# A block of attention mixers and a mixture of experts on one core: two more places for streamed weights, and another order in the experts' one-chunk items

## The reference, cut to what matters

```python
def moe_swiglu(h, router_w, w_gate, w_up, w_down):      # h: 256 x 1024
    logits = (h @ router_w).astype(jnp.float32)          # 8 experts
    top_logit, top_idx = lax.top_k(logits, TOP_K)        # TOP_K = 2
    gate = jax.nn.softmax(top_logit, axis=-1)
...
    def expert_block(args):
        tok, e = args
        xb = h[tok]
        hid = jax.nn.silu(xb @ w_gate[e]) * (xb @ w_up[e])   # 1024 x 3584 each
        return hid @ w_down[e]                               # 3584 x 1024
...
    return jnp.zeros_like(h).at[row_token].add(y)
```

## The kernel before

| item | 0 | 1 | 2 | 3 | 4 | 5 | 6 | 7 | 8 | 9 | 10 |
|---|---|---|---|---|---|---|---|---|---|---|---|
| chunks | both | 0 | both | both | both | 1 | 0 | 1 | 1 | both | 0 |
| groups | 3 | 1 | 3 | 3 | 3 | 1 | 4 | 1 | 4 | 3 | 1 |

## Time and profile before

### The profile page before, as it was taken

How to read it: one execution, slowest core, us unless ns; L and a number is a source line. 1 busy time by engine, 2 the same in 40 slices (tenths; PEclk the granted TensorE clock), 3 DMA queues, 4 the chain that set the end, 5 groups by cost and what they waited for, 6 DMA issues and landing times.

```text
span 2036.8 us, 44518 instructions
## 1 busy us (share of the span) xinstructions
PE 1910.4 (94%) x19574; PEld 1226.8 (60%) x19574; DVE 757.2 (37%) x1757; ACT 332.6 (16%) x772; POOL 292.3 (14%) x266
## 2 busy tenths in 40 slices
PE   6999988999999999999988899799999999999995
PEld 4886556578888888886777645235344453544352
DVE  5586547346553554436566510110100110111102
ACT  3005635121000000213453300000000000000001
POOL 0872614000000000076341000000000000000000
PEclk8999989999999999999899799999999999999997
DMA  9224672422213222321202799999999999999995
GB/s 355 84 83 151 222 248 86 167 82 83 84 63 104 83 83 78 131 83 42 83 2 86 296 354 393 411 418 414 418 419 418 419 396 421 371 415 397 369 406 246
DMA packets 134573, 481.93 MB, mean 237 GB/s; under 512 B 11770, under 2 KB 48490, under 8 KB 103530
## 3 DMA queue, kind: packets, MB, share of 16 engines
q1 hardware_dynamic: 129904, 473.99, 59.8%
q0 software_dynamic: 928, 3.15, 0.5%
q10 hardware_dynamic: 3546, 1.91, 0.3%
HBM read 476.92 MB, written 2.10 MB: 235 GB/s over the span
## 4 chain that ended last, share of the span: by engine, by line
PE 69%; DMA 3%; POOL 3%; DVE 3%; ACT 1%; issue 1%; DVEq 0%; SPq 0%; ACTq 0%; POOLq 0%
PE bank L837 67%; DMA ring<-in_moe_w_dram 3%; PE bank L840 2%; POOL ring L3644 2%; POOL work L3646 1%; DVE gates L3561 1%; ACT ring L1965 1%; POOL work L3642 0%; DVE hT L3565 0%; ACT L1965 0%; DVE small L2767 0%; DVE ring L2948 0%; DVE ring L2967 0%; DVE ring L2824 0%; DVE ring L2977 0%
## 5 line engine op out<-in xcount | busy, mean ns | idle before, releaser
L837 PE MATMUL bank<-ring,hT 128*32 128x256 f32 (+3 forms) x9664 | 790.1, 472 | 34.8 <-DMA ring<-in_moe_w_dram 19.5
L837 PEld LDWEIGHTS bank<-ring,hT 128*32 128x32 f32 (+1 forms) x9664 | 343.8, 113 | 468.6 <-issue 330.6
L837 PE MATMUL bank<-ring 64*64 64x64 f32 (+5 forms) x4184 | 420.3, 298 | 31.2 <-ACT ring L1965 11.3
L837 PEld LDWEIGHTS bank<-ring 64*64 64x64 f32 (+3 forms) x4184 | 345.1, 161 | 92.6 <-issue 46.5
L837 PE MATMUL bank<-hT,ring 128*128 128x256 f32 (+1 forms) x1448 | 363.4, 407 | 6.0 <-DMA ring<-in_w_in_dram 2.8
L837 PEld LDWEIGHTS bank<-hT,ring 128*128 128x128 f32 x1448 | 278.0, 194 | 75.8 <-issue 35.0
L1965 ACT ACTIVATE gates<-bank 128x256 f32<-128x256 f32 (+2 forms) x75 | 36.2, 484 | 704.3 <-PE bank L837 686.6
L3561 DVE TENSOR_TENSOR gates<-gates,bank 128x512 f32<-128x512 f32 (+1 forms) x42 | 25.1, 597 | 280.3 <-PE bank L837 280.3
L3584 DVE COPY work<-bank 128x512 f32<-128x512 f32 (+1 forms) x18 | 9.4, 554 | 279.9 <-PE bank L837 279.9
L3726 POOL DMA_INDIRECT table<-token_rows,moe_index x10 | 9.2, 921 | 705.6 <-PE bank L840 580.8
L3546 DVE SCALAR_TENSOR_TENSOR xT<-bank,mods,xT 128x256 f32<-128x256 f32 x88 | 35.5, 476 | 178.7 <-PE bank L837 178.7
(11 more groups left out here) (268 smaller groups left out, 1403.0 us busy)
## 6 DMA issues: line engine op xcount, KB each, us to landing
ring<-in_moe_w_dram SPq DMA_DIRECT2D x240, 1024.0 KB, 19.7
ring<-in_moe_w_dram SPq DMA_DIRECT2D x128, 768.0 KB, 16.7
ring<-in_ada_w_dram SPq DMA_DIRECT2D x24, 2048.0 KB, 7.9
ring<-in_ffn_w_dram SPq DMA_DIRECT2D x22, 1024.0 KB, 7.6
ring<-in_w_in_dram SPq DMA_DIRECT2D x10, 2048.0 KB, 8.9
ring<-in_w_out_dram SPq DMA_DIRECT2D x4, 2048.0 KB, 9.5
ring<-in_ffn_w_dram SPq DMA_DIRECT2D x4, 1536.0 KB, 6.3
ring<-in_ffn_w_dram SPq DMA_DIRECT2D x4, 1280.0 KB, 5.8
```

Source lines behind the costliest of these rows:

```text
L837: return nc.tensor.matmul(o, w, x, start=start, stop=stop)
```

## The change

- `fixed_places` (new) puts each piece into the ring or into one of two **side places** of 8 KB a partition, whichever comes free earlier by the count of used pieces. The two are `work[:, 0:2 * D]` (where `hrow`, the rows for item 0's gather, lay) from the first used piece on, and `spare` from the 17th used piece on.
- SP waits for the store of `hrow` to `token_rows` ahead of the first piece that goes to `work`.
- `fetched` is now one buffer in `work`. GpSimd fetches item u's rows when item u - 1's rows have been turned.
- `pick` moves to `tmpA`, and a scratch of the routing to `cond`.
- One-chunk items: TensorE does `turn_spread` and `next_rows` ahead of the down; `next_rows` waits for the first two groups' products and no longer for all. VectorE makes the picks ahead of `multiply(0)`.
- All items: the first piece of a down goes group by group, each group's matmuls behind a wait for that group alone.
- A count of 20 semaphores for the pieces, where it was 19; the loop for overflowing experts, which doesn't run with these inputs, loads `hrow` again.

```diff
-PIECE_SEMS = 19
+PIECE_SEMS = 20
+SIDE_FREE = (1, 2 * DT + 1)
...
-        pick = work[:, 3072:3328]
-        wpick = work[:, 3328:4352]
-        spread = work[:, 4352:5376]
+        wpick = work[:, 3072:4096]
+        spread = work[:, 4096:5120]
+        fetched = work[:, 5120:6144]
+        pick = tmpA[:, 256:512]
...
-        def fetched(u):
-            return spare[:, u % 2 * D:u % 2 * D + D]
+        side = (work[:, 0:2 * D], spare)
...
+        def fixed_places(order):
+
+            got, at, free = [], RING_FROM, list(SIDE_FREE)
+            for n, (kind, c, b) in enumerate(order):
+                size = words(kind, c)
+                if at % RING + size > RING:
+                    start = at + RING - at % RING
+                else:
+                    start = at
+                need = max((k + 1 for k, (where_to, lo, _) in enumerate(got) if where_to is None and lo < start + size - RING), default=0)
+                s = free.index(min(free))
+                if free[s] < need:
+                    got.append((s, 0, free[s]))
+                    free[s] = n + 1
+                else:
+                    got.append((None, start, need))
+                    at = start + size
+            return got
...
                     else:
+                        if first_item and n == first_in_rows:
+                            sp.wait_ge(rows_stored, 32)
                         sp.wait_ge(moe_used, before_load(u, n))
...
-                        if b == 0:
-                            pe.wait_ge(moe_hidT_ready, done0 + (i + 1) * G)
...
-                        for q in range(2):
-                            for g in range(G):
-                                for s in range(4):
...
+                        by_group = [(q, g) for g in range(G) for q in range(2)]
+                        for q, g in by_group if b == 0 else sorted(by_group):
+                            if (b, q) == (0, 0):
+                                pe.wait_ge(moe_hidT_ready, done0 + (i * G + g + 1))
+                            for s in range(4):
...
-                        pe.wait_ge(moe_hid_ready, done0 + len(cs) * G)
+                        pe.wait_ge(moe_hid_ready, done0 + (len(cs) - 1) * G + min(G, 2))
...
-                    down(0, {4: turn_spread, 5: next_rows})
+                    turn_spread()
+                    next_rows()
+                    down(0)
...
+                if len(cs) == 1:
+                    next_picks()
                 multiply(0)
...
-                if u > 2:
-                    pool.wait_ge(moe_gathered, 2 * (u - 1))
-                g.indirect_dma_start(fetched(u)[0:n, :], None, token_rows,
+                if u > 1:
+                    pool.wait_ge(moe_gathered, 2 * u)
+                g.indirect_dma_start(fetched[0:n, :], None, token_rows,
```

More of the change, by code:

```diff
@@ L614, in used_up @@
             return sum(start < place[n][1] - RING for start, _ in place[:n])
+        def fixed_places(order):
[15 more added lines that the diff above has]
+            return got
         fixed_order = [piece for _, chunks in PLAN for piece in stream(chunks)]
-        fixed_place = places(fixed_order, RING_FROM)
+        fixed_place = fixed_places(fixed_order)
         FIXED = len(fixed_order)
         assert FIXED == EXPERTS * NPIECE
-        assert all(used_up(fixed_place, n) > n - PIECE_SEMS for n in range(FIXED))
         spill_place = places(stream(WHOLE), 0)
@@ L636, in memory @@
         def memory(u, n):
-            start, end = fixed_place[pieces_before(u) + n] if is_static(u) else spill_place[n]
-            return ring[:, start % RING:start % RING + end - start]
+            if not is_static(u):
+                start, end = spill_place[n]
+                return ring[:, start % RING:start % RING + end - start]
+            at = pieces_before(u) + n
+            in_side, start, _ = fixed_place[at]
+            size = words(*fixed_order[at][0:2])
+            return ring[:, start % RING:start % RING + size] if in_side is None else side[in_side][:, 0:size]
         def before_load(u, n):
             if is_static(u):
-                return used_up(fixed_place, pieces_before(u) + n)
+                at = pieces_before(u) + n
+                return max(fixed_place[at][2], at - PIECE_SEMS + 1, 0)
             return pieces_before(u) + used_up(spill_place, n)
@@ L806, in _ @@
             assert sorted(2 * SLOT + base for base in (0, 8192, GDIR, GDIR + 8192)) == \
-                sorted(fixed_place[n][0] % RING for n in UNREAD)
+                sorted(fixed_place[n][1] % RING for n in UNREAD)
+            first_in_rows = [place[0] for place in fixed_place].index(0)
             for u in range(STATIC):
@@ L816, in _ @@
                     e = sp.value_load(ints[0:1, bass.ds(o + EXPERTS, 1)], min_val=0, max_val=EXPERTS - 1)
+                    sp.wait_ge(moe_used, pieces_before(o + STATIC))
+                    sp.dma_start(hrow, token_rows.rearrange("(t p) n -> p t n", p=P)).then_inc(rows_stored, 16)
                     expert(o + STATIC, e)
@@ L1944, in _ @@
                     pe.wait_ge(moe_hid_ready, multiplied_before(o + STATIC))
+                    pe.wait_ge(rows_stored, o * 16 + 48)
                     gather(o + STATIC)
@@ L3567, in multiply, with next_picks @@
                         ins.then_inc(moe_hidT_ready, 1)
+                def next_picks():
+                    weighted_picks(u)
+                    picks(u + 1)
+                    dve.wait_ge(moe_picks, u * 4 + 6)
+                    dve.sem_inc(moe_sel_ready, 1)
                 if deferred:
                     add_rows(u - 1)
+                if len(cs) == 1:
+                    next_picks()
                 multiply(0)
```

30 lines of the change are left out of this document (14 added, 16 removed).

## The result

The changed kernel takes 2018.49 us (median of 12 executions, 2014.94 to 2026.66) against 2027.78 us for the kernel before (12 executions, 2026.12 to 2038.85). The ratio is 0.9944, 95% interval 0.9930 to 0.9958: 11.4 us less, between 8.5 and 14.2. Predicted were 14.7 us less. Two later comparisons gave 0.9949 and 0.9944.

What follows compares the result with a forecast made beforehand. Bound: the weights' stream held while the ring is full. First stretch 5.05 plus second set 9.6 us made 14.7 us off the median of 2027.9, so 2013.2 us, range 2004.5 to 2021.5.

Steps and rivals of the forecast that it cites:

- What bounds the kernel: Experts' part from 1159 us: what counts is the time the weights' stream is held because the ring is full.
- First stretch, 5.05 us: Item 0, 1161 to 1227 us: two side places return 5.05 us of a 10.7 us loss.
- Second set, 9.6 us: Lossy stretches from 1764 to 1956 us: places' 5.05 plus TensorE's 7.6 us of relief return all 9.6 us.
- The turns, 7.6 us: Items 6 to 8: transposes ahead of the down remove 7.6 us of TensorE's waits ahead of the first down piece.
- the clock's 2.9: Behind item 8's wait: without the wait the half-speed clock goes too, 2.9 us, a bonus outside the sum.
- Nothing for the single buffer, the picks and the wait for `hrow`: One buffer for fetched rows, VectorE's earlier picks and the wait for `hrow`'s store: each costs nothing.
- the first, that all losses go: Both sets of losses: places return more than their bytes, up to 20.3 us, giving 2007.6 us; chance 0.14.
- no change: Lossy stretches: their rate is the memory's own and not the ring's, so 2027.9 us; chance 0.08.
- slower: The single buffer makes TensorE wait for rows; over 1% slower means above 2048 us; chance 0.03.
- The second: Second set: TensorE's waits turn into others, only places pay, 7.6 to 10.1 us, so 2018 to 2020; chance 0.18.
- The signs: 1161 to 1227 at about 375 GB/s, none under 405 from 1760, transposes' waits under 1 us, last landing 14 to 15 earlier.
- the signs of being wrong: TensorE waits for picks or rows, a lossy stretch staying behind 1860, or the last stretch of transfers entered later.

Runs made afterwards that it cites:

- two places fewer: The kernel before, with SP waiting for two used pieces more ahead of each load, taking two places off its ring: 2044.72 us, ratio 1.0064.
- the turns alone: The changed kernel without its two side places, all its one-chunk item changes kept: 2023.66 us, ratio 0.9958 to the kernel before.
- the places alone: The changed kernel with turns, picks and first down piece as in the kernel before; side places and single row buffer stay: 2025.14 us, ratio 0.9981.
- two sums left: The changed kernel with five of seven index sums moved from item 0 to item 1, second side place opening at piece 63: 2016.58 us, ratio 0.9931.

## Why the prediction was right or wrong

- **What bounds the kernel**: right. The stream's holds set the time; two places fewer, two more, and work off TensorE all moved the last landing by way of them.
- **First stretch, 5.05 us**: the term that was mis-sized; it measured 2.3 to 2.6 us at piece 61. The step that failed is "From 1227 to 1764 the stream runs freely, so the gain is kept". The gain was made, 5.0 us at piece 39, and half of it was lost again by piece 61. Behind it stands "Two places more put it 2 x 2.53 = 5.05 us ahead": for pieces 42 and 45 to 56 the places let SP issue one piece earlier and not two, and one piece is 2.53 us. There the stream isn't free of TensorE: item 0's down frees a piece every 2.59 us (the steady interval between used pieces), the free stream takes one in 2.53, and a piece of the changed kernel lands a median of 7.6 us after its issue between 1233 and 1252,

```profile
DMA to landing us min/median/max: 6.6/7.6/7.9
```

  where at 1316, with the queue full, it is 29.1. So the stream follows the releases at nearly its own rate. The kernel before is in the same state (first line, 1237 to 1257), and so is the kernel with two places fewer (second line, 1228 to 1248), whose pieces land some 5 us later:

```profile
DMA to landing us min/median/max: 9.0/9.3/9.8
DMA to landing us min/median/max: 6.8/8.0/8.5
```

  With two places fewer this time is not longer, so it doesn't tell how much a place can return. That the lost piece of the ring is the cause is worked out from the places and fits all the kernels above; a ring in which both places count at every piece was not run, and it would be the test. How much of the loss the holds of some 2 us around pieces 53 and 54 make up is open.
- **Second set, 9.6 us**: right in size. Piece 230 to 343: 270.4 before, 260.4 to 261.1 after. How it is shared was half right: the turns alone reach all of it (10.4), the places alone 3.9, together no more than the turns. The sum needed 2.0 us of the places' 5.05 beside the turns' 7.6 to fill 9.6; the runs show that it needed none, because the clock's share came on top of the turns.
- **The turns, 7.6 us, and the clock's 2.9**: right. TensorE is 9.9 us faster from piece 230 to piece 298 in the first traces (7.7 and 10.7 between the second trace of before and the other two of the changed kernel), the waits are down by 7.6 us, and the clock doesn't fall behind items 6 and 8 in any of the three. The prediction saw one wait of two followed by half the clock and took it for a bonus; the second trace of before has it behind both (below), with the same 6.8 us at half speed in all. At the start of item 8 TensorE now waits for weights instead (1.5 us at 1788.48), which costs nothing, since the stream is what counts: the second trace, whose clock falls behind that wait, has the last landing where the first has it (840.3 against 840.5).
- **Nothing for the single buffer, the picks and the wait for `hrow`**: right as far as the traces show. No wait of TensorE for fetched rows appears in the changed kernel's list, and its 0.3 us for L3594 in item 7 are for the product.
- **The rivals**: the first, that all losses go, is out, and so are no change and slower. The second, at 7.6 to 10.1 us by the places alone, is near the total by number (the medians, 9.3 us apart, lie in it), but for the wrong reason: it is the first set and not the second that fell short.
- **The signs**: item 0's rate rose as said (379 GB/s), and the waits fell as said. Two signs failed: a stretch behind 1760 stays under 405 (361 GB/s from 1759 to 1768), and the last landing is 12.9 us earlier and not 14 to 15. None of the signs of being wrong appeared: item 9's stretches are at 416 and 412 GB/s, and the last stretch of transfers begins at 1972.84 and not at 1994.02.
- **The single number**: 2013.2 predicted, 2018.5 measured, 14.7 against 11.4 us by the ratio. The first term accounts for 2.5 to 2.8 of the 3.3 us; the rest is inside the interval.

## What to carry to other kernels

Before you price more buffers by their bytes, work out for each transfer which use releases it, before and after. Pieces of two sizes in a ring can waste at its end what a side buffer adds, and a buffer that is there on paper is then missing where the stream needs it. A stretch at the full rate isn't by that a stretch with room: compare the rate at which the consumer frees places with the stream's own, and where they are nearly the same (2.59 and 2.53 us here), work taken off the consumer counts too. When two remedies address the same loss, try each by itself: here the turns alone gave 8.5 of the 11.4 us and the places alone 3.9.

## What the runs showed of the hardware

Behind the same 3.2 us of idle time TensorE's clock fell in item 8 in the first trace and not in item 6. The second trace of the kernel before has it behind both, at half the granted clock (first line item 6, second line item 8):

```profile
1733.90:1736.90 3.00, 3.00 (x32) 1.48 (x28) 0.55 (x3) 0.00 (x0) 0.00 (x0) 0.50 1.02 416
1832.80:1835.90 3.10, 2.87 (x28) 1.38 (x32) 1.54 (x6) 0.00 (x0) 0.00 (x0) 0.50 1.02 423
```

The kernels with two places fewer and with the places alone show the same, so it is seven of eight such waits. The time at half speed differs from wait to wait (6.8 us behind item 8 in the first trace, 3.4 behind each in the second), but in each of the four traces it is 6.8 us in all, worth 2.9 to 3.4 us of work. In the changed kernel a wait of 2.2 us for weights at the start of item 8 was followed by half the clock in the second trace, and the 1.5 us in the first were not. So a single dip in one trace is a draw, and only several traces give a price. In item 0 the small matmuls of one column come ahead of a fall of the clock in every trace but two of the kernels that do all seven sums there: piece 17 is done after 43.9 us without it, 44.7 to 44.9 with a short fall and 46.8 with a longer one. With two sums left there was none (41.7 us). The Trainium skill ("TensorE: Matmul & The Clock Gate", Part 1) ties the clock to the array's recent activity; the runs agree in that much.

Executions of one and the same program differed by 10 us ahead of the experts' part: item 0's first piece was used at 1151.4, 1157.4 and 1161.7 us in three traces of the changed kernel, while from there to the last landing they took 840.3, 840.5 and 841.4. Two traces should be laid against each other from a common event.
